# Four insertions of the head steps moved to stand beside others, and the order of three engines around them

## The reference, cut to what matters

```python
z = rms_norm(x, g_mix) @ w_in          # q | k | v | forget logits | lru x | lru gate
# attention, per head; F is the cumulated log forget value
s = q @ k.T * HEAD_DIM**-0.5 + F_query - F_key     # causal mask
att = softmax(s) @ v                   # decode tokens: over 2048 cached keys and values, in 16 pages
# recurrence, per block
xc = causal_conv(lru_x, w_conv)        # width 4
r, i = sigmoid(xc @ wa + ba), sigmoid(xc @ wx + bx)
a = exp(-8 * r * softplus(-lam)); b = sqrt(1 - a**2) * i * xc
h[t] = a[t] * h[t-1] + b[t]; lru = gelu(lru_gate) * h
x = x + concat(rms_norm(att, g_att), rms_norm(lru, g_lru)) @ w_out
x = x + relu(rms_norm(x, g_ffn) @ w_up)**2 @ w_down          # then a final RMSNorm
```

## Time and profile before

| | |
|---|---|
| median of three runs | 2304.42 us |
| the profiled execution | 2305.47 us, its span 2303.9 us |
| mean granted TensorE clock | 0.993 |
| PE busy | 2252.2 us, 98% of the span |
| DVE busy | 1605.5 us, 70% |
| ACT busy | 858.1 us, 37% |
| DMA | 368.47 MB, 160 GB/s in the mean |

### The profile page before, as it was taken

How to read it: one execution, slowest core, us unless ns; L and a number is a source line. 1 busy time by engine, 2 the same in 40 slices (tenths; PEclk the granted TensorE clock), 3 DMA queues, 4 the chain that set the end, 5 groups by cost and what they waited for, 6 DMA issues and landing times.

```text
span 2303.9 us, 50021 instructions
## 1 busy us (share of the span) xinstructions
PE 2252.2 (98%) x19889; PEld 2202.1 (96%) x19889; DVE 1605.5 (70%) x2043; ACT 858.1 (37%) x1201; POOL 154.6 (7%) x194
## 2 busy tenths in 40 slices
PE   7999999999999999999999999999999999999997
PEld 7999898989988999999999999999999999999997
DVE  7349889888884697876576576576576576576563
ACT  5124433434354333343343243243243243243245
POOL 0001111111104031000000000000000000000002
PEclk8999999999999999999999999999999999999998
DMA  7457999999985243333433433433433433433422
GB/s 238 106 159 260 323 327 329 305 311 327 319 285 185 97 135 88 108 103 102 128 101 100 129 98 100 131 97 100 132 95 100 134 94 100 136 92 100 137 87 98
DMA packets 386972, 368.47 MB, mean 160 GB/s; under 512 B 12259, under 2 KB 350596, under 8 KB 385844
## 3 DMA queue, kind: packets, MB, share of 16 engines
q1 hardware_dynamic: 359828, 295.38, 41.7%
q0 software_dynamic: 18608, 67.64, 8.2%
q10 hardware_dynamic: 8448, 4.20, 0.6%
HBM read 354.22 MB, written 12.94 MB: 159 GB/s over the span
## 4 chain that ended last, share of the span: by engine, by line
PE 86%; DVE 7%; DVEq 2%; issue 2%; ACT 1%; DMA 1%; ACTq 0%; SPq 0%
PE PS L1897 36%; PE PS L1901 18%; PE PS L2343 9%; PE PS L2342 9%; PE PS L2341 9%; DVE KR L1350 2%; PE PS L2058 2%; DVEq L1508 1%; DVE SC L1352 1%; PE PS L2106 1%; DVE WL L1214 1%; PE PS L2248 1%; PE PS L2096 0%; ACT WH L744 0%; DVE NM L1507 0%
## 5 line engine op out<-in xcount | busy, mean ns | idle before, releaser
L1094 ACT ACTIVATE WH<-RAW 128x1024 fp32r<-128x1024 f32 x293 | 304.7, 1056 | 680.9 <-PE PS L1901 521.5
L1648 DVE TENSOR_TENSOR WL<-RAW,WH 128x1024 fp32r<-128x1024 f32 x293 | 358.3, 1223 | 133.7 <-ACT WH L1094 131.8
L1897 PE MATMUL PS<-XH,WH 128*128 128x260 f32 x1952 | 407.0, 290 | 10.8 <-DVE XL L1279 5.9
L1897 PE MATMUL PS<-HH,WH 128*128 128x260 f32 x2048 | 412.4, 282 | 1.4 <-DVE HL L1653 0.7
L1901 PE MATMUL PS<-HH,WL 128*128 128x260 f32 x2048 | 411.7, 282 | 0.0
L1897 PE MATMUL PS<-HL,WH 128*128 128x260 f32 x2048 | 410.8, 282 | 0.0
L1901 PE MATMUL PS<-XH,WL 128*128 128x260 f32 x1952 | 394.8, 284 | 0.0
L1897 PE MATMUL PS<-XL,WH 128*128 128x260 f32 x1952 | 394.6, 284 | 0.0
L1751 DVE TENSOR_TENSOR A<-A,PS 128x520 f32<-128x520 f32 x256 | 177.4, 696 | 264.3 <-PE PS L1901 263.5
L1897 PEld LDWEIGHTS PS<-XH,WH 128*128 128x128 f32 x1952 | 303.0, 190 | 22.6 <-issue 13.3
L1897 PEld LDWEIGHTS PS<-HH,WH 128*128 128x128 f32 x2048 | 314.6, 188 | 2.1 <-issue 1.1
(11 more groups left out here) (335 smaller groups left out, 3087.5 us busy)
## 6 DMA issues: line engine op xcount, KB each, us to landing
KR<-in_cache_k POOLq DMA_DIRECT2D x128, 512.0 KB, 6.0
VR<-in_cache_v SPq DMA_DIRECT2D x128, 512.0 KB, 6.3
RAW<-in_w_up SPq DMA_DIRECT2D x128, 512.0 KB, 4.2
RAW<-in_w_down SPq DMA_DIRECT2D x128, 512.0 KB, 4.4
RAW<-in_w_in SPq DMA_DIRECT2D x82, 512.0 KB, 8.4
RAW<-in_w_out SPq DMA_DIRECT2D x32, 512.0 KB, 5.3
TMP<-in_w_up SPq DMA_DIRECT2D x30, 512.0 KB, 6.2
xT_spill<-A SPq DMA_DIRECT2D x1, 4160.0 KB, 16.5
```

Source lines behind the costliest of these rows:

```text
L1094: nc.scalar.activation(RING_H[SLOT[i]], RB[b], ACT.Copy).then_inc(f_hi, 1)
L1648: V.tensor_tensor(RING_L[SLOT[i]], RB[op_block(i)], RING_H[SLOT[i]].bitcast(F32), ALU.subtract).then_inc(f_lo, 1)
L1897: mm(dsts[c], wh(k), x[:, k, c * HT:(c + 1) * HT], start=first and n == 0 and x is xh, stop=False)
```

## The change

It moves pieces of work in the orders of three engines; no instruction is added or taken away, and none has another size.

- TensorE: `max_all` from (0, 25) to (0, 21); `transpose_probs` from (2, 7) to (2, 21); `attend` from (2, 19) to (3, 7), ahead of `rows`; the gates' products from behind unit q = 3 to (3, 21). Where `values` have the same place, they come first.
- ScalarE: in `gates` the `split_hi` of U_L+1 moves from ahead of tanh to behind exp, and the broadcast query's copy (L929) from ahead of the square root to behind it; `attended` moves behind `split_hi` of U_L+4.
- VectorE: in steps 1 to 7 `conv` and `split_lo` of U_L+4 move ahead of the key pages 12 and 13.

```diff
--- before.py
+++ after.py
@@ -859,7 +859,7 @@
 
             act.wait_ge(state_ready, 2)
 
-            def gates(h, after_sigmoids, between):
+            def gates(h, next_hi, broadcast_query):
 
                 act.wait_ge(gates_ps, h + 1)
                 ba, bx = PRM[:, one(R_BA + h)], PRM[:, one(R_BX + h)]
@@ -867,14 +867,14 @@
                 nc.scalar.activation(PR[:, SEQ:T], PS[:, 6, 0:NB], ACT.Sigmoid, bias=ba)
                 nc.scalar.activation(PR[:, T:T + SEQ], PS[:, 5, :], ACT.Sigmoid, bias=bx)
                 nc.scalar.activation(PR[:, T + SEQ:2 * T], PS[:, 6, NB:2 * NB], ACT.Sigmoid, bias=bx).then_inc(sig_done, 1)
-                after_sigmoids()
                 act.wait_ge(sig_done, h + 1)
                 nc.scalar.activation(PT[:, 0:T], PR[:, 0:T], ACT.Tanh, scale=CPOS[:, one(h)])
                 nc.scalar.activation(PR[:, 0:T], PR[:, 0:T], ACT.Exp, scale=CNEG[:, one(h)]).then_inc(decay_done, 1)
-                between()
+                next_hi()
 
                 act.wait_ge(ratio_ready, h + 1)
                 nc.scalar.activation(PT[:, 0:T], PT[:, 0:T], ACT.Sqrt).then_inc(root_done, 1)
+                broadcast_query()
 
             def probabilities(h):
 
@@ -963,8 +963,6 @@
                 if head:
                     rows_out(tile_wait(U_L + 1, 2 * i), vT, VS, i)
                     split_hi(U_L + 3, 2 * i)
-                if prev:
-                    attended(i - 1)
                 if head:
                     slot = tile_wait(U_L + 2, 2 * i)
                     if prev:
@@ -975,6 +973,8 @@
                     nc.scalar.activation(XW[:, W3 + SEQ:].rearrange("p (b j) -> p b j", j=CW)[:, :, W3],
                                          PS[:, 2 * slot + 1, HB:HT], ACT.Copy).then_inc(tile_out[slot], 1)
                     split_hi(U_L + 4, 2 * i)
+                    if prev:
+                        attended(i - 1)
 
                     for tr, tok, ready, stored, bank, dst in ((ktr_ps, ktok, ktok_ready, k_out, 5, new_k_p),
                                                               (vtr_ps, vtok[:, :, :], vtok_ready, v_out, 6, new_v_p)):
@@ -1473,15 +1473,12 @@
                 if head:
                     score(i, range(10, 12))
                 if head:
-                    if prev:
-                        score(i, range(12, 14))
                     conv(i)
                     if final:
                         head_lo(NH)
                         head_lo(NH + 1)
                     split_lo(U_L + 4, 2 * i)
-                    if not prev:
-                        score(i, range(12, 14))
+                    score(i, range(12, 14))
                 if head and not final:
                     last_scores(i)
 
@@ -2202,41 +2199,7 @@
                     ins.then_inc(vtr_ps, 1)
 
 
-                extra = {}
-                if head:
-                    if not prev:
-                        extra[1, 5] = other_rows
-                    extra[0, 13 if prev else 5] = queries
-                    extra[3, 7] = rows
-                if prev:
-                    extra[0, 15] = lambda: max_rows(i)
-                    extra[0, 25] = lambda: max_all(i)
-                    extra[1, 5] = head_scores
-                    extra[2, 7] = lambda: transpose_probs(i - 1)
-                    extra[2, 19] = lambda: attend(i - 1)
-
...
-                if head:
+                def gate_sums():
 
                     pe.wait_ge(gw_full, 32 * (i + 1))
                     pe.wait_ge(conv_done, i + 1)
@@ -2249,6 +2212,41 @@
                     for g in range(2):
                         ins = mm(PS[:, 6, g * NB:(g + 1) * NB], GW[:, g, :], XC[:, SEQ:T], start=True, stop=True)
                     ins.then_inc(gates_ps, 1)
+
+                extra = {}
+                if head:
+                    extra[3, 21] = gate_sums
+                    if not prev:
+                        extra[1, 5] = other_rows
+                    extra[0, 13 if prev else 5] = queries
+                    extra[3, 7] = (lambda: (attend(i - 1), rows())) if prev else rows
+                if prev:
+                    extra[0, 15] = lambda: max_rows(i)
+                    extra[0, 21] = lambda: max_all(i)
+                    extra[1, 5] = head_scores
+                    extra[2, 21] = lambda: transpose_probs(i - 1)
+
...
```

More of the change, by code:

```diff
@@ L2202, in rows @@
                     ins.then_inc(vtr_ps, 1)
+                def gate_sums():
+                    pe.wait_ge(gw_full, 32 * (i + 1))
+                    pe.wait_ge(conv_done, i + 1)
+                    if prev:
+                        pe.wait_ge(att_ready, i)
+                    pe.wait_ge(ktok_ready, i + 1)
+                    pe.wait_ge(vtok_ready, i + 1)
+                    for g in range(2):
+                        mm(PS[:, 4 + g, :], GW[:, g, :], XC[:, 0:SEQ], start=True, stop=True)
+                    for g in range(2):
+                        ins = mm(PS[:, 6, g * NB:(g + 1) * NB], GW[:, g, :], XC[:, SEQ:T], start=True, stop=True)
+                    ins.then_inc(gates_ps, 1)
                 extra = {}
                 if head:
+                    extra[3, 21] = gate_sums
                     if not prev:
@@ L2238, in step @@
                         unit(U_L + q, 2 * i, U_L + q, 2 * i, insert)
-                if head:
-                    pe.wait_ge(gw_full, 32 * (i + 1))
-                    pe.wait_ge(conv_done, i + 1)
-                    if prev:
[L2244 to L2251, removed]
             pe.wait_ge(cum_ready, 3)
```

## The result

| | median, us | runs |
|---|---|---|
| kernel before | 2304.20 | 8, 2301.89 to 2305.88 |
| changed kernel | 2311.01 | 8, 2309.74 to 2312.51 |

The ratio is 1.0032, with a 95% interval of 1.0021 to 1.0042: slower by 6.8 us. The forecast was 2310.6. The profiled execution of the changed kernel took 2312.51 us, its span is 2310.9, 7.0 more than that of before, and the granted clock is 0.989.

The account below looks back on a forecast made before the run. TensorE, busy 98% of the span, was taken to bound the kernel. -15.0 + 15.1 - 2.9 + 1.9 = -0.9, plus 7.1 for the clock, gave +6.2 us: 2310.6 us, range 2301 to 2317.

Parts of the forecast that it names:

- The wait that goes: Transposes' waits for VectorE's normalising in seven head steps go wholly: 13.5 us, with step 1's clock 15.0 us less.
- The wait that comes: Unit q = 3 on TensorE waits for its weights' low part, seven steps at 2.16 us: +15.1 us.
- The clock: 1.2 GHz behind 4.7 of the seven new pauses, at 1.54 us each: +7.1 us, bounds 0 to 10.8.
- The interruptions: TensorE's head steps: cheaper `max_all` and fewer slow first pairs, 2.9 us less; gates' wait for the convolution costed at nothing.
- ScalarE's order: Behind step 7: copy ahead of the square root's table load makes root and last recurrent row later, +1.9 us.
- The drain: Behind step 7: the skill page's drain of about 1.38 us on the table load; tail 3.3 instead of 1.9, not summed.

Follow-up runs that it names:

- both ways of giving ScalarE's copy an earlier start: Two runs on the changed kernel: transposes at (2, 13), 2296.06 us; ScalarE's high part of unit q = 3's weights ahead of the transposed probabilities' copies, 2297.80 us.
- the fill: Changed kernel with nine unused matmuls more on TensorE in each step from 1 on, behind unit q = 2's last slice: 2304.24 us.
- the moved transposes: Changed kernel with the transposes of the probabilities at (2, 13) instead of (2, 21): 2296.06 us.

## Why the prediction was right, point by point

- **The wait that goes** was right: no wait of the transposes is left. That it could have gone for less was missed. I had seen VectorE's 0.98 us for `max_all` and that it would come earlier, but weighed it only against the new wait, where it is idle time. By itself, with the transposes where they were, this is worth 9.0 us.
- **The wait that comes** was right in mechanism and size: 1.94 or 1.95 shown seven times, where "about 1.95" was forecast, and both ways of giving ScalarE's copy an earlier start take most of it away in steps 2 to 7. In step 1 they don't, because VectorE is level with the copy there. The prediction had the two level in every step (446.95 and 446.9) and found slack for VectorE in `max_all`'s move; in step 1 there was none.
- **The clock** was right as a share: 5 falls of 7 against the 4.7 forecast, at 1.5 us each, and the fill shows that they carry the loss. That the share came out as forecast is luck, though. Over the four kernels with this same pause 16 of 28 were followed by a fall (5, 4, 4 and 3 of 7), so 57%, not the 67% that three pauses of the trace had given. With three falls the changed kernel would have been within 0.2%. The Trainium skill's page "TensorE: Matmul & The Clock Gate" (Why this matters for your kernels) warns only of idle gaps longer than these; the traces here don't agree, since pauses of 1.94 us cost the clock more often than not.
- **The interruptions** were about right: a step without a fall gained 0.16 us where the terms gave 0.44 + 1.94 - 2.16 = 0.22. TensorE never waited for the convolution at the gates.
- **ScalarE's order** had the right number by the wrong step. The step read: "But the copy then stands ahead of the square root's table load ... the root, and the last recurrent row behind it, come 1.93 - 0.25 + a remainder of 0.2 = 1.9 us later." They don't come later after the unit's end; TensorE comes sooner, by the 2.08 us of its gates. Right number, wrong cause: that is luck too. I had counted both shifts of ScalarE against TensorE's time and put the remainder on the copy, which merely changed its place in a chain of fixed length. Measured from one event, the end of the unit, the copy would have dropped out at once. The drain that the prediction weighed beside this term doesn't show: in the changed kernel the load ends at 683.21 + 1.28 = 684.49 and the root starts at 684.50.
- **Not in the sum**: the longer half clock behind that wait (3.78 us long, not 2.12) and one more fall behind the last values, whose waits are 2.2 in one piece instead of 3.1 in three. Each is about 1.5 us. Smaller waits at the tail took 1.7 back (0.8 at the maximum, 0.9 at the pages). So the forecast of +6.2 came near the 6.8 partly because what it left out nearly cancels.

The sum made afterwards, by the trace: -13.5 for the old waits and +15.1 for the new, as forecast; -2.7 for the interruptions (a step without a fall gained 0.16 = 1.94 - 2.16 + 0.38, so 0.38 a step); +1.7 at the last row and -1.7 at the small waits; and falls for eight times 1.5 where before has two (five in the loop, a double one behind the last row's wait, one behind the values), +9.0. That is 7.9 us; the spans differ by 7.0. Most of that gap lies ahead of the head steps: the same matmul stands at 81.86 us in the changed kernel and at 82.48 in the one before, 0.6 earlier, and over the profiled runs it stands anywhere from 81.24 to 83.77.

## What to carry to other kernels

When a wait is to be removed by moving its consumer, look first at what the producer waits for: here one small matmul two slices earlier gave 9 us alone, and moving the consumer as well turned the gain into a loss. Whatever is put behind a moved step on another engine must be followed to its own next user; here the copy of the next weights stood behind the copies of the transposes' result. Compare chains from one common event, and not from the time at which an engine that has itself shifted arrives.

## What the runs showed of the hardware

- The same pause of 1.94 us is followed by 1.2 GHz in one step and not in the next, with the same work around it: 16 of 28 times. Of five pauses of 1.84 to 1.86, over all the traces, three were and two were not; one of 1.78 was. One of 1.58 with another of 0.68 behind it was, one of 1.68 with 0.72 behind it was not. No pause of 1.76 or less that stood alone was, and there are 15 from 1.49 up. Longer ones are no surer up to 2.12: of five from 2.04 to 2.12 four were, and one of 2.12 was not; all those of 2.21 and of 3.78 to 3.89 were.
- Idle time on TensorE and lost clock can be traded for useless work: nine matmuls (1.17 us) in a pause of 1.94 left the next unit's start where it was and brought back 6.8 us over seven steps. This repairs the clock, not the wait; the moved transposes, which take away most of both, brought 15 us.
